# Hybrid decoder layer on one core: head 2's queries and scores placed between V rows 4 to 9, unit 2's routing two groups later, head 0's score copies ahead of two exponentials

## The chip, the cores and the metric

The kernel runs on one core of one Trainium2 chip. The metric is the device time of one execution in microseconds (us), as the median of several runs. TensorE multiplies, ScalarE applies functions and copies, VectorE does element-wise work and reductions, GpSimd here builds tables and issues the gathers, SyncE issues the plain loads. 16 DMA engines carry out the transfers of all of them.

## What is computed

One decoder layer on 256 tokens of width 1024, in float32. First a norm, a combined projection, and two kinds of attention side by side (8 heads of block attention, 4 of differential attention), an output projection and the residual. Then a second norm and the part that takes most of the time, a feed-forward layer of 16384 single-neuron experts:

```python
q = (xc @ w_query).reshape(PEER_CHUNK, PEER_HEADS, 2, PEER_D_HALF)
sc = jnp.einsum('chpd,hpnd->chpn', q, sub_keys)
s1, i1 = lax.top_k(sc[:, :, 0], PEER_TOPK)
s2, i2 = lax.top_k(sc[:, :, 1], PEER_TOPK)
cand = s1[..., :, None] + s2[..., None, :]
...
best, pos = lax.top_k(cand, PEER_TOPK)
g = jax.nn.softmax(best, axis=-1)
h = jax.nn.gelu(jnp.einsum('cd,chkd->chk', xc, u[experts]), approximate=False)
return jnp.einsum('chk,chkd->cd', h * g, v[experts])
```

Each token has 8 heads, and each head picks 16 experts: from two score vectors of 128 keys the best 16 each, from their sums the best 16 pairs. For each expert a row of `u` (1024 numbers) is multiplied with the token's vector, and a row of `v` is added to the result with the weight `gelu(...) * g`.

## The kernel before

The 256 tokens are two halves of 128, which lie on the 128 partitions. The work of the expert layer is cut into 16 **units** (half times head), each of 16 **rows**: row n of the 256 is one gathered tile of U (128 partitions x 1024, each partition its own expert's row, 512 KB) and one of V. Four rows are a **group**, so there are 64 groups, four to a unit. U tiles lie in a ring of 10 buffers, V tiles in a ring of 9.

Every engine has a program of its own, written out by hand in order, and each runs strictly in that order; semaphores join them. For the expert layer these are the steps:

- TensorE, `query(e)` (L1279): 8 matmuls (16 in the trace, which counts two passes for each) make half of a head's query, from the weights `wq[e // 2]`; `key_scores(e)` (L1274) multiplies it with the 128 keys. Event e is head e // 2 of the first half of the tokens for e under 16. `head_queries(i)` (L1294) does both events of head i in one piece: it is called for heads 0, 1 and 2 before the loop over V rows (L1363); later heads stand between V rows.
- ScalarE copies the query out of PSUM (`query_evac`, L656) for `key_scores`, and the scores for VectorE (`scores_evac`, L647). It also does the exponentials of the attention (`exponentials(b)`, L543; batches 4 to 11 belong to the second half of the tokens), the gelu of a group (`gelu(g)`, L696, on four dot products), and for each row the diagonal matrix of its weights (`diagonal(n)`, L702; a ring of 8).
- VectorE turns scores into expert numbers, in three parts (`route(u, part)`, L1004): the top keys, the top candidates, the expert numbers (`expert_ready`) and softmax inputs. It makes the dot products of a group (`dots(g)`, L1016), which wait for their U rows and free their buffers (`u_used`), and the group's weights from gelu and softmax (`weights(g)`, L1027), one group later. x is read from SBUF in groups 0 to 2 and from PSUM afterwards.
- GpSimd issues the gathers (L463): in turn g the four U rows of group g (at the start of a unit it waits for that unit's experts; each row waits for its buffer), and then the four V rows of group g - 2, which wait for V buffers freed by TensorE (`v_used`).
- TensorE multiplies each V row with its diagonal (L1372), adding into the output banks.
- SyncE loads the query weights in four portions (L396 to L404). `wq[2]` and `wq[3]` overwrite `v_sb` and `soft`, which the attention of the second half still reads, so their loads wait for its last values product (`values_done`). `wq[4]` to `wq[7]` wait for the last output projection of the second half, whose steps stand between V rows 11 to 22.

Around the change ScalarE's program for the start of the loop is: exponentials 10 and 11, two copies of probabilities, x into PSUM, squares and square root for the second half's attention output (`d_squares`, `d_deviation`), the copies of head 2's queries and scores (L721 to L724), and then `gelu(0)`. VectorE's is: routing of unit 0, attention work, `dots(0)`, first part of routing unit 1, `dots(1)`, `weights(0)`, the other two parts of unit 1, `dots(2)`, `weights(1)`, first part of unit 2. The whole loop waits for nothing else on GpSimd's side than expert numbers and free buffers.

## Time and profile before

| | us |
|---|---|
| median of 3 runs | 840.93 (838.71 to 841.11) |
| the profiled execution, as timed | 836.34 |
| its span from the first to the last instruction | 834.5 |
| TensorE busy | 679.0 (81%) |
| VectorE busy | 525.5 (63%) |
| ScalarE busy | 236.6 (28%) |
| GpSimd busy | 502.4 (60%) |
| gathers of U and V (268.47 MB), share of 16 DMA engines | 81.5% of the span |
| mean TensorE clock granted | 0.943 |

The page cuts the span into 40 equal slices of 20.9 us and gives for each the busy share of every engine, the granted clock, and the bytes that the DMA engines moved. Busy shares are averages over stages that have different limits, so a change is read from the stage in which it stands: which engine waits there, for whom, and what that engine waits for itself. In a timeline row the number in brackets is the idle time of the engine before the instruction, with the one that released it. POOL is GpSimd, DVE is VectorE, ACT is ScalarE, PE is TensorE.

### The profile page before, as it was taken

How to read it: one execution, taken by the hardware profiler on the slowest of the kernel's cores; microseconds unless marked ns; L12 is line 12 of the kernel's file. 1: busy time of each engine (PE TensorE's matmuls, PEld its weight loads, DVE VectorE, ACT ScalarE, POOL GpSimd, SP SyncE). 2: the span in 40 equal slices, each digit the busy share in tenths (PEclk: the TensorE clock that was granted, in tenths of full speed). 3: DMA queues.
4: the chain of work that ended last, by engine and by line, in shares of the span. 5: the costliest groups of instructions: out<-in, count | busy, mean ns of one | idle time of the engine just before them, and what ended most of it. 6: DMA issues, size and time to landing. Idle time of an engine off the chain costs nothing.

```text
span 834.5 us, 7478 instructions
## 1 busy us (share of the span) xinstructions
PE 679.0 (81%) x2205; PEld 369.6 (44%) x2205; DVE 525.5 (63%) x1389; ACT 236.6 (28%) x606; POOL 502.4 (60%) x533
## 2 busy tenths in 40 slices
PE   5999997469978988878888989887776667777776
PEld 4877575435435444335444445443332223333332
DVE  5565169279652867576667676657666757665454
ACT  7567244232311432311212222331212121212110
POOL 5000007447773777777777767777777776777751
PEclk9999998599997999999999999999999999999999
DMA  8955108949999999999999999999999999999994
GB/s 326 310 166 185 53 1 305 376 143 404 409 403 390 400 409 409 407 409 410 408 409 409 409 409 409 411 409 409 409 410 408 410 409 409 409 409 409 409 409 180
DMA packets 92121, 297.91 MB, mean 357 GB/s; under 512 B 8737, under 2 KB 17074, under 8 KB 92082
## 3 DMA queue, kind: packets, MB, share of 16 engines
q0 software_dynamic: 73728, 268.47, 81.5%
q1 hardware_dynamic: 18354, 28.98, 10.1%
q8 instruction: 18, 0.29, 0.1%
q14 instruction: 21, 0.17, 0.1%
HBM read 296.36 MB, written 1.05 MB: 356 GB/s over the span
## 4 chain that ended last, share of the span: by engine, by line
DMA 34%; PE 34%; POOL 15%; issue 7%; DVE 6%; ACT 4%; DVEq 0%; SPq 0%; POOLq 0%; ACTq 0%
DMA v_row<-in_peer_v_dram,expert 23%; PE bank L1372 16%; POOL u_row L446 9%; DMA u_row<-in_peer_u_dram,expert 7%; POOL v_row L457 6%; PE xg L1119 5%; PE bank L1290 4%; DMA wq<-in_peer_w_query_dram 3%; PE bank L1244 3%; DVE u_row L1023 2%; PE bank L1185 1%; PE bank L1168 1%; ACT soft L549 1%; DMA x_sb<-in_x_dram 1%; ACT L700 0%
## 5 line engine op out<-in xcount | busy, mean ns | idle before, releaser
L1372 PE MATMUL bank<-v_row,diag 128*128 128x512 f32 x1000 | 475.7, 622 | 110.8 <-DMA v_row<-in_peer_v_dram,expert 94.7
L1023 DVE CUSTOM_DVE_ANT_0 u_row<-u_row,xg 128x1024 f32<-128x1024 f32 x244 | 296.4, 1220 | 186.2 <-DMA u_row<-in_peer_u_dram,expert 178.5
L1372 PEld LDWEIGHTS bank<-v_row,diag 128*128 128x128 f32 x1000 | 189.3, 198 | 353.9 <-issue 320.1
L446 POOL DMA_INDIRECT u_row<-in_peer_u_dram,expert x256 | 246.4, 962 | 148.0 <-DVE expert L999 70.5
L457 POOL DMA_INDIRECT v_row<-in_peer_v_dram,expert x256 | 241.2, 942 | 113.3 <-issue 56.6
L1290 PE MATMUL bank<-featT,wq 128*128 128x128 f32 x512 | 68.8, 294 | 23.1 <-DMA wq<-in_peer_w_query_dram 22.2
L1290 PEld LDWEIGHTS bank<-featT,wq 128*128 128x128 f32 x512 | 68.3, 210 | 38.0 <-DMA wq<-in_peer_w_query_dram 23.2
L700 ACT ACTIVATE h_gelu<-h_dot 128x4 f32<-128x4 f32 x64 | 12.8, 202 | 251.8 <-DVE h_dot L1023 251.7
L707 ACT ACTIVATE diag<-ident,act_w 128x128 f32<-128x128 f32 x250 | 82.5, 389 | 3.6 <-DVE act_w L1036 3.6
L660 ACT ACTIVATE qT<-bank 128x128 f32<-128x128 f32 x32 | 8.9, 277 | 176.7 <-PE bank L1290 176.7
L356 POOL TENSOR_TENSOR normed<-qk_raw,t_qk_rs 128x512 f32<-128x512 f32 x4 | 4.1, 1047 | 56.6 <-DVE t_qk_rs L896 56.6
L795 DVE TENSOR_TENSOR w_lo<-w_raw,w_hi 128x2048 fp32r<-128x2048 f32 x12 | 27.8, 2327 | 7.5 <-ACT w_hi L493 7.5
L1036 DVE TENSOR_TENSOR act_w<-h_gelu,gate 128x4 f32<-128x4 f32 x64 | 10.3, 161 | 35.0 <-ACT h_gelu L700 34.4
L1119 PE MATMUL xg<-w_hi,xn_hi 128*128 128x512 f32 x72 | 29.5, 410 | 2.0 <-ACT qk_raw L529 2.0
L1244 PE MATMUL bank<-w_raw,mixT 128*128 128x512 f32 x64 | 29.6, 593 | 0.0
L1119 PE MATMUL xg<-w_hi,xn_lo 128*128 128x512 f32 x72 | 28.9, 401 | 0.0
L1119 PE MATMUL xg<-w_lo,xn_hi 128*128 128x512 f32 x72 | 28.6, 398 | 0.0
L654 ACT ACTIVATE scores<-bank 128x128 f32<-128x128 f32 x32 | 8.7, 276 | 67.4 <-PE bank L1277 67.4
L493 ACT ACTIVATE w_hi<-w_raw 128x2048 fp32r<-128x2048 f32 x12 | 22.9, 1922 | 4.9 <-DMA w_raw<-in_w_in_dram 2.3
L957 DVE MAX8 key_val<-scores 128x8 f32<-128x128 f32 x64 | 15.4, 282 | 11.0 <-ACT scores L654 11.0
L700 ACT ACT_TABLE_LOAD x17 | 21.8, 1283 | 0.3
L1023 DVE DVE_READ_ACCUMULATOR2_ANT h_dot<- 128x1 f32 x256 | 21.1, 82 | 0.0
(160 smaller groups left out, 518.0 us busy)
## 6 DMA issues: line engine op xcount, KB each, us to landing
w_raw<-in_w_in_dram SPq DMA_DIRECT2D x12, 1024.0 KB, 7.9
wq<-in_peer_w_query_dram SPq DMA_DIRECT2D x8, 1024.0 KB, 18.1
w_raw<-in_w_out_dram SPq DMA_DIRECT2D x4, 1024.0 KB, 5.1
u_row<-in_peer_u_dram,expert POOLq DMA_INDIRECT x256, 16.5
v_row<-in_peer_v_dram,expert POOLq DMA_INDIRECT x256, 16.6
x_sb<-in_x_dram SPq DMA_DIRECT2D x2, 512.0 KB, 3.8
g_row<-in_norm_g_dram SPq DMA_DIRECT2D x1, 512.0 KB, 12.9
out_dram<-y_rows SPq DMA_DIRECT2D x1, 512.0 KB, 6.7
```

The source lines that it names most:

```text
L446: pool.indirect_dma_start(u_rows[n % U_RING][:, :], None, peer_u[0], bass.IndirectOffsetOnAxis(ap=expert[:, u, s:s + 1], axis=0))\
L457: pool.indirect_dma_start(v_rows[n % V_RING][:, :], None, peer_v[0], bass.IndirectOffsetOnAxis(ap=expert[:, u, s:s + 1], axis=0))\
L493: act.activation(w_hi[:, j % W_PARTS, :, :].rearrange("p k n -> p (k n)"), w_raw[:, j % W_LOADS, :], ACT.Copy)\
L700: act.activation(h_gelu[:, u % 4, s:s + GROUP], h_dot[:, u % 4, s:s + GROUP], ACT.Gelu).then_inc(gelu_done, 1)
L707: act.activation(diag[:, m % DIAG_RING, :], ident[:, :], ACT.Copy, scale=act_w[:, u % 4, s:s + 1])\
L795: dve.tensor_tensor(w_lo[:, j % W_PARTS, :, :].rearrange("p k n -> p (k n)"), w_raw[:, j % W_LOADS, :], w_hi[:, j % W_PARTS, :, :].rearran ...
L957: at[a] = mark(dve.max(key_val[:, r2, a, top], score[a]))
L1023: dve.tensor_tensor_reduce(out=row[:, :], in0=row[:, :], in1=x_of, scale=1.0, scalar=0.0, op0=ALU.mult, op1=ALU.add, accum_out=h_dot[:, u ...
L1119: ins = mm(ps[bank][:, :], a[:, 4 * kh + k, h * P:(h + 1) * P], b[:, j % W_PARTS, k, :], start=kh == 0 and k == 0 and n == 0, stop=kh == 1 ...
L1244: ins = mm(ps[y_bank(h, c)][:, :], mixT[h][:, 4 * kh + k, :], w_raw[:, j % W_LOADS, k * COLS:(k + 1) * COLS], start=False, stop=last)
L1290: ins = mm(ps[2 + e % 2][:, 0:P], wq[i][:, k, c * P:(c + 1) * P], featT[h][:, k, :], start=k == 0, stop=k == KD - 1)
L1372: ins = mm(ps[y_bank(h, c)][:, :], diag[:, m % DIAG_RING, :], v_rows[n % V_RING][:, c * COLS:(c + 1) * COLS], start=False, stop=True, skip ...
```

## The change

Three things move; nothing is added or left out.

1. `head_queries(2)` goes away before the loop over V rows. TensorE now does `query(4)` behind V row 4, `query(5)` behind row 6, `key_scores(4)` behind row 7 and `key_scores(5)` behind row 9. ScalarE's four copies go behind the diagonals of rows 6, 8, 9 and 11, two rows later than on TensorE, as it is done for later heads.
2. The routing of unit 2, one part in each of the turns 2, 3 and 4 of VectorE's loop, now has its first part in turn 4 and the other two in turn 5.
3. `exponentials(4)` stands behind the copies of head 0's scores instead of ahead of them.

```diff
--- before.py
+++ after.py
@@ -667,9 +667,9 @@
             skT_evac(1)
             query_evac(0)
             query_evac(1)
-            exponentials(4)
             scores_evac(0)
             scores_evac(1)
+            exponentials(4)
             exponentials(5)
             act.wait_ge(late_v_done, 1)
             act.activation(v_sb[:, 0, 1, :], ps[5][:, :], ACT.Copy).then_inc(copied, 1)
@@ -718,10 +718,6 @@
                 act.activation(xg[:, c, :], scaled[:, 0, c * COLS:(c + 1) * COLS], ACT.Copy).then_inc(xg_in_psum, 1)
             d_squares(1)
             d_deviation(1)
-            query_evac(4)
-            query_evac(5)
-            scores_evac(4)
-            scores_evac(5)
             for g in range(GROUPS + 1):
                 if g < GROUPS:
                     gelu(g)
@@ -743,6 +739,15 @@
                             feat_evac(1, 0)
                             feat_evac(1, 1)
                         u, at = divmod(n - 2, TOPK)
+                        if u == 0:
+                            if at == 4:
+                                query_evac(4)
+                            if at == 6:
+                                query_evac(5)
+                            if at == 7:
+                                scores_evac(4)
+                            if at == 9:
+                                scores_evac(5)
                         if 0 <= u <= 4:
                             e = 2 * (u + 3)
                             if at == 10:
@@ -1074,8 +1079,13 @@
                 if g == 12:
                     x2_rstd(1)
                 u, at = divmod(g - 2, UNIT_GROUPS)
-                if 0 <= u and at < 3 and u + 2 < UNITS:
+                if 0 < u and at < 3 and u + 2 < UNITS:
                     route(u + 2, at)
+                if g == 4:
+                    route(2, 0)
+                if g == 5:
+                    route(2, 1)
+                    route(2, 2)
             weights(GROUPS - 1)
 
             for k, n in enumerate(ADDED_ROWS):
@@ -1344,7 +1354,6 @@
             soft_transposes(8, 11)
             values(7, 10)
             values(8, 11)
-            head_queries(2)
 
             def out_step(step):
 
@@ -1389,6 +1398,14 @@
                     x2_transposes(1)
                 if n == 57:
                     pe.wait_ge(featT_ready[0], 3)
+                if n == 4:
+                    query(4)
+                if n == 6:
+                    query(5)
+                if n == 7:
+                    key_scores(4)
+                if n == 9:
+                    key_scores(5)
                 if u <= 4:
                     e = 2 * (u + 3)
                     if at == 10:
```

The line numbers behind the change are higher by 5 to 10 than before.

On TensorE, at the end of the attention and the start of the V rows, before (the L1290 row is head 2's query, L1372 a V row):

```order
L1168 MATMUL bank<-v_sb,probsT 128x64 x8
L1155 MATMUL xg<-ident,soft 128x128 x8
L1168 MATMUL bank<-v_sb,probsT 128x64 x8
L1290 MATMUL bank<-featT_121,wq_128 128x128 x16
L1277 MATMUL bank<-skT,qT 128x128 x2
L1372 MATMUL bank<-v_row_144,diag 128x512 x2
L1372 MATMUL bank<-v_row_145,diag 128x512 x2
```

and now, from V row 3 on (L1300 is `query`, L1287 a score product, L1243 transposes, L1381 a V row; rows 0 to 2 stand right behind the values product):

```order
L1381 MATMUL bank<-v_row_147,diag 128x512 x2
L1381 MATMUL bank<-v_row_148,diag 128x512 x2
L1300 MATMUL bank<-featT_121,wq_128 128x128 x8
L1381 MATMUL bank<-v_row_149,diag 128x512 x2
L1381 MATMUL bank<-v_row_150,diag 128x512 x2
L1300 MATMUL bank<-featT_121,wq_128 128x128 x8
L1381 MATMUL bank<-v_row_151,diag 128x512 x2
L1287 MATMUL bank<-skT,qT 128x128
L1381 MATMUL bank<-v_row_152,diag 128x512 x2
L1243 MATMUL bank<-ident,scaled 128x128 x8
L1381 MATMUL bank<-v_row_144,diag 128x512 x2
L1287 MATMUL bank<-skT,qT 128x128
```

Head 2's block ahead of the V rows is gone, and its query stands in two halves behind V rows 4 and 6, its scores behind rows 7 and 9.

On ScalarE, at the end of the attention's work and the start of the groups, before (L566 is the square root, L660 and L654 the copies of queries and scores, L700 gelu, L707 diagonals):

```order
L561 ACTIVATE scaled<-bank 128x512
L566 ACT_TABLE_LOAD
L566 ACTIVATE t_d_sd<-t_d_ms 128x4
L660 ACTIVATE qT<-bank 128x128 x2
L654 ACTIVATE scores_123<-bank 128x128 x2
L700 ACT_TABLE_LOAD
L700 ACTIVATE h_gelu<-h_dot 128x4 x2
L707 ACTIVATE diag<-ident,act_w 128x128 x4
L700 ACTIVATE h_gelu<-h_dot 128x4
L707 ACTIVATE diag<-ident,act_w 128x128 x4
```

and now:

```order
L561 ACTIVATE scaled<-bank 128x512
L566 ACT_TABLE_LOAD
L566 ACTIVATE t_d_sd<-t_d_ms 128x4
L700 ACT_TABLE_LOAD
L700 ACTIVATE h_gelu<-h_dot 128x4 x2
L707 ACTIVATE diag<-ident,act_w 128x128 x4
L700 ACTIVATE h_gelu<-h_dot 128x4
L707 ACTIVATE diag<-ident,act_w 128x128 x3
L660 ACTIVATE qT<-bank 128x128
L707 ACTIVATE diag<-ident,act_w 128x128
L694 ACT_TABLE_LOAD
```

The gelu of group 0 and the diagonals of rows 0 to 3 come directly behind the square root, and the first copy for head 2 behind the diagonal of row 6.

On ScalarE, at head 0's queries and scores, before (L549 are exponentials):

```order
L660 ACTIVATE qT<-bank 128x128 x2
L549 ACT_TABLE_LOAD
L549 ACTIVATE soft,t_sums<-soft,t_nmax 128x256 x2
L654 ACTIVATE scores_123<-bank 128x128 x2
L549 ACTIVATE soft,t_sums<-soft,t_nmax 128x256 x2
```

and now:

```order
L660 ACTIVATE qT<-bank 128x128 x2
L654 ACTIVATE scores_123<-bank 128x128 x2
L549 ACT_TABLE_LOAD
L549 ACTIVATE soft,t_sums<-soft,t_nmax 128x256 x4
```

The two score copies have moved ahead of the table load and all four exponentials.

## Rows read from the trace of the kernel before

**Rows 1.** The page: GB/s in its slices, and one group of instructions on VectorE
```profile
GB/s 326 310 166 185 53 1 305 376 143 404 409 403 390 400 409 409 407 409 410 408 409 409 409 409 409 411 409 409 409 410 408 410 409 409 409 409 409 409 409 180
...
L1023 DVE CUSTOM_DVE_ANT_0 u_row<-u_row,xg 128x1024 f32<-128x1024 f32 x244 | 296.4, 1220 | 186.2 <-DMA u_row<-in_peer_u_dram,expert 178.5
```

**Rows 2.** Windows of three stretches: busy by engine, clock, DMA share, GB/s
```profile
core 0: us, PE busy (x) PEld busy (x) DVE busy (x) ACT busy (x) POOL busy (x), PEclk, DMA share, GB/s
160.00:165.00 5.00, 2.37 (x11) 2.37 (x12) 0.00 (x0) 0.00 (x0) 0.00 (x0) 0.50 1.03 394
165.00:190.00 25.00, 18.52 (x56) 9.83 (x56) 18.29 (x64) 8.11 (x20) 10.34 (x10) 0.90 0.56 182
190.00:230.00 40.00, 40.00 (x127) 20.43 (x126) 32.36 (x96) 11.05 (x32) 30.24 (x33) 1.00 1.03 409
```

**Rows 3.** Timeline of GpSimd: start, us, instruction, idle time before it
```profile
125.32 1.19 POOL L446 DMA_INDIRECT u_row<-in_peer_u_dram,expert  x1 [52.48 <-DVE expert L999]
...
157.91 0.94 POOL L457 DMA_INDIRECT v_row<-in_peer_v_dram,expert  x1 [0.30 <-issue]
...
176.91 0.93 POOL L446 DMA_INDIRECT u_row<-in_peer_u_dram,expert  x1 [18.07 <-DVE expert L999]
...
179.79 1.99 POOL L446 DMA_INDIRECT u_row<-in_peer_u_dram,expert  x1 [0.30 <-issue]
...
218.35 0.94 POOL L446 DMA_INDIRECT u_row<-in_peer_u_dram,expert  x1 [0.30 <-issue]
...
237.04 0.93 POOL L457 DMA_INDIRECT v_row<-in_peer_v_dram,expert  x1 [0.34 <-PE bank L1372]
```

**Rows 4.** Timelines of ScalarE and VectorE, 150 to 177 us
```profile
150.68 0.20 ACT L566 ACTIVATE t_d_sd<-t_d_ms 128x4 f32<-128x4 f32 x1
...
169.56 1.28 ACT L700 ACT_TABLE_LOAD   x1
...
171.16 0.16 DVE L1036 TENSOR_TENSOR act_w<-h_gelu,gate 128x4 f32<-128x4 f32 x1 [20.33 <-ACT h_gelu L700]
...
176.47 0.18 DVE L999 SCALAR_TENSOR_TENSOR expert<-pair_idx 128x16 uint32<-128x16 f32 x1
```

**Rows 5.** Timeline of TensorE: head 2's queries, V rows 4 on, half queries
```profile
162.63 5.74 PE L1290 MATMUL bank<-featT,wq 128*128 128x128 f32 x32 [12.19 <-DMA wq<-in_peer_w_query_dram]
...
182.70 10.55 PE L1372 MATMUL bank<-v_row,diag 128*128 128x512 f32 x20 [3.76 <-ACT diag L707]
...
197.40 1.95 PE L1290 MATMUL bank<-featT,wq 128*128 128x128 f32 x16
...
199.18 1.88 PE L1372 MATMUL bank<-v_row,diag 128*128 128x512 f32 x4
...
254.50 3.78 PE L1290 MATMUL bank<-featT,wq 128*128 128x128 f32 x16 [10.01 <-DMA wq<-in_peer_w_query_dram]
```

**Rows 6.** Landing: query weights 2; the last two; V 155-160 us; U 125-131 us
```profile
DMA to landing us min/median/max: 12.1/12.1/12.1
...
DMA to landing us min/median/max: 39.5/39.7/39.8
...
DMA to landing us min/median/max: 9.6/10.3/11.0
...
DMA to landing us min/median/max: 4.6/5.2/6.1
```

**Rows 7.** Timelines of ScalarE and VectorE around head 0's scores, and head 2's second
```profile
113.40 0.28 ACT L660 ACTIVATE qT<-bank 128x128 f32<-128x128 f32 x1 [1.51 <-PE bank L1290]
...
119.72 0.60 ACT L675 ACTIVATE v_sb<-bank 128x512 f32<-128x512 f32 x1 [2.33 <-PE bank L1119]
...
169.26 0.28 ACT L654 ACTIVATE scores<-bank 128x128 f32<-128x128 f32 x1 [0.35 <-PE bank L1277]
...
116.50 0.49 DVE L957 MAX8 key_val<-scores 128x8 f32<-128x128 f32 x2 [2.90 <-ACT scores L654]
...
124.22 0.18 DVE L999 SCALAR_TENSOR_TENSOR expert<-pair_idx 128x16 uint32<-128x16 f32 x1
```

## The prediction

> **What bounds the kernel now.** I read the slices of the page first, to see when which resource is full. From about 190 us to 815 us the transfers move 390 to 411 GB/s, mostly 409, in every slice [rows 1]: that stretch is bound by the DMA engines, at 0.5243 MB (128 x 1024 x 4 bytes) / 409 GB/s = 1.28 us for a gathered row of U or V. Such a stretch gets shorter only by starting earlier or by losing a gap. There is one gap: the slice at 167 to 188 us stands at 143 GB/s [rows 1]. Cut out by windows, 165 to 190 us moved 182 GB/s instead of 409, so 25 x (1 - 182/409) = **13.9 us of transfer time are missing** [rows 2].
>
> Next I asked who starved the queue. GpSimd issues all gathers, in program order. After v7 at 157.91 us it idles 18.07 us until u16, released by expert numbers from VectorE [rows 3]. VectorE itself sat 20.33 us at its first activation weights, for the gelu of group 0 on ScalarE [rows 4]. ScalarE had its last square root done at 150.88 us; next in its program stand the copies of head 2's queries and scores, and only behind them the gelu, whose table load began at 169.56 us [rows 4]. TensorE's query(4) waited for query weights 2: 12.19 us, to 162.63 us [rows 5]. These weights overwrite values still read by the last values product, so their load can only be issued at 150.5 us, and it took 12.1 us beside the gathers [rows 6]. So one late load holds ScalarE, through it VectorE, through it GpSimd, and in the end all transfers, although no U row of unit 1 needs head 2's query.
>
> **Part 1: head 2's queries move behind V rows 4 to 9.** Nothing is removed: 32 query matmuls, 4 score matmuls and 4 copies are still there. Now after the square root ScalarE loads the gelu table and runs gelu. Before, table load to activation weights was 169.56 to 171.16 = 1.60 us [rows 4], so the weights come at 150.88 + 1.60 = 152.5 us, 18.7 us earlier. Candidates and experts of unit 1 follow in 176.65 - 171.16 = 5.5 us [rows 4], to 158.0 us. GpSimd is done with v7 at 158.85 us. The wait of 18.07 us vanishes, down to the 0.3 us between gathers.
>
> What is late next? The transfers issued by then still need time: a gather issued at 155 to 160 us landed after 10.3 us against 5.2 us in the stream's first 6 us [rows 6]. I take the smallest landing there, 4.6, as unloaded and the largest, 11.0, as loaded: **6.4 us of queued work** cover small delays of GpSimd. The next 32 gathers took from 176.91 to 218.35 us, 41.4 us [rows 3], for 32 x 1.28 = 41.0 us of transfer, so the cover stays about constant. u16 to u19 need dot products 6 to 9: the first eight are done when VectorE's wait begins, at 150.8 us [rows 4], the next two come 18.7 us earlier, like the weights. I take the whole gap as gained: **-13.9 us**. Its ends: no gain at all if the wait merely finds a new place (a rival below), and 17.8 us (the whole wait of GpSimd less 0.3) if transfers followed the issues one for one. The value stays at the missing bytes, since the transfers, not the issues, set the end.
>
> **The dot products beside the gathers.** The dot products of group 2 still read x from SBUF and run while u16 to u19 are issued; beside them one gather took 1.99 us instead of 0.93 [rows 3], 1.1 us more, which the 41.4 us contain. The Trainium skill (GPSIMD Engine Reference, Specifications) says that GpSimd's SBUF interfaces are shared with VectorE and that VectorE instructions with two SBUF inputs contend. Taken strictly, all four gathers would pay the 1.1 us, 3.2 us more than here, and unhidden the sum would be 12.6 us instead of 15.8; by the rows the cost is the 1.1 us, and hidden. The trace agrees with the rule in kind, not for all four.
>
> **Part 2: unit 2's routing two groups later.** It needs head 2's scores, which now hang behind V row 9. V row 4 began at 182.70 us once its diagonal was there [rows 5]; 18.7 us earlier is 164.0. From there to the second score product TensorE has 6 V rows, two queries, eight transposes and two small products. A V row is 1.7 us (x4 row, 1.88 with its drain), a query half of 16 matmuls 1.8 [rows 5]: 10.3 + 3.6 + 1.3 (12 small matmuls at a sixteenth of a half query) = 15.2 us, and 2 us more because the five rows of before took 10.55 instead of 8.6 us as the clock rose [rows 5]. Scores at 181.2, copied 181.8. V rows 8 and 9 land before that, since their gathers follow u16's, which comes at 158.3 us (158.0 and the issue) instead of 176.91, 18.6 us earlier. VectorE then needs the key tops (three parts took 116.50 to 124.40 = 7.9 us [rows 7], less 5.5 = 2.4), four dot products of 1.22 us [rows 1] and 5.5 us for the other two parts: experts of unit 2 at 181.8 + 12.8 = 194.6 us. GpSimd wants them for u32 at 158.3 + 41.4 = 199.7 us, and with the cover 206.1 would do. VectorE may wait some 6 us for the scores; cost 0, hidden by 5 us in GpSimd's order and 6.4 us of queued transfers. If that cover were gone, each us late would cost one.
>
> **Part 3: TensorE and the V ring.** From V row 4 at 182.70 us TensorE works nearly without a gap [rows 2, 5], and at 237.04 us v31 takes the slot of V row 22, for which GpSimd had waited 0.34 us [rows 3]. That is 54.3 us; the change puts 4.0 us into it (two queries, two scores). Row 22: 164.0 + 54.3 + 4.0 = 222.3 us; GpSimd wants it at 237.04 - 18.6 = 218.4. It waits 3.9 us, under the cover of 6.4: cost 0, but this is the thinnest cover of all. Load waits at the later query weights go with it: the four loads are issued behind V row 22's neighbours, as before.
>
> **Part 4: head 0's scores ahead of the exponentials.** Before, ScalarE copied the two scores after a table load and two exponentials, and VectorE idled 2.90 us until 116.50 [rows 7]. Now the first copy follows the query copy of 113.40 + 0.28, ends near 113.9, and the second starts 0.35 us later for the score product (the gap at 169.26 us is that product) [rows 7]: 114.25 to 114.5, and VectorE starts near 114.6, 1.9 us earlier, and so do the experts of unit 0 and the first gather, at 125.32 us before [rows 3]. GpSimd's other gate there, the late value product, ends at 119.7 us, before the experts of 122.5, and stays hidden. The exponentials come about 0.8 us later, hidden by ScalarE's idle time of 2.33 us before 119.72 [rows 7]. The stream starts 1.9 us earlier and is full: **-1.9 us**, between 0 (if it only lengthens a queue) and 2.9 (the whole idle time). I gave part 1 none of this head start.
>
> **Sum.** 13.9 + 1.9 = 15.8 us. The profiled execution took 836.34 us (span 834.5), so 820.5 for it; the median of the three runs, 840.93, lies 4.6 us above it, and with that gap kept: **825.1 us**.
>
> **Rivals.**
> (a) *The clock takes it back.* At 160 to 165 us the granted clock was 0.50, the 1.2 GHz level, after 12 us without matmuls [rows 2]; before, the query block ran there and the V rows after it at 2.4 GHz. Now V rows 0 to 3 come first, then a wait for the next diagonal. A half query took 3.78 us at the low level against 1.95 [rows 5]. If all work from row 4 to 9 runs low, it costs 15.2 us more: row 22 at 237.5 against 218.4 + 6.4 = 224.8, a loss of 12.7 us, so 837.8 us. Against it: before, the clock was back within 5.7 us of query matmuls. The Trainium skill (TensorE: Matmul & The Clock Gate, Part 1) says that the throttled clock is the default and activity lifts it; by that rule the thin V rows 0 to 3 would leave TensorE low, which is this rival. Chance 0.06; half its price lies inside my range.
> (b) *Head 0 brings nothing*, because something else holds GpSimd's first gather or the head start is lost before 160 us: 827.0. Chance 0.10.
> (c) *The wait only changes its name.* ScalarE or VectorE meets another wait before unit 1's experts, and GpSimd stays at u16 until about 177 us: 840.9. Every operand on that path is done by 150.9 us in the trace, so 0.04.
> (d) *Slower: head 2's weights land late.* Place: query(4) behind V row 4, now with an uninterrupted gather stream beside the load. From landing to unit 2's experts I count 27 us: 13.5 on TensorE (15.2 less V row 4), then 0.6 and 12.8. Landing by 179 us is harmless (206.1 - 27); from 195 us on the idle time eats all 15.8 us. The load took 12.1 us beside the same gathers, but the last of four took 39.8 us [rows 6], which from 150.5 gives 190.3 and still a gain of 4.6. Beyond that it turns over: at 50 us, 200.5, it is 21.4 - 15.8 = +5.6, 846.5 us. For speaks the fuller queue, against that the first of its group took 12.1 us, and that V rows would stop being issued and give way. Chance 0.03.
>
> **Numbers.** Forecast 0.77, (a) 0.06, (b) 0.10, (c) 0.04, (d) 0.03. The range begins at 821.0, where GpSimd's whole 17.8 us and 1.9 would count (821.2), and ends at 832.0, which takes in (b), half of (a) and what is lost if the thin cover of part 3 is gone (3.9 us) together with the 2 us of clock. A measurement of this kernel can tell about 0.3%, 2.5 us, from no change: faster 0.93 (forecast, (a), (b)), same 0.04, slower 0.03.
>
> **What would show it.** The slices hold 400 GB/s and more from 155 us on, with no hole. GpSimd has no wait over 4 us before u32, the first gather is issued near 123.4 us, the weights of group 0 come near 152 us, ScalarE's wait for the first query of head 2 remains but releases nobody. VectorE waits some 6 us for head 2's scores near 180 us. The forecast is wrong if GpSimd shows a new wait of over 6.4 us for expert numbers or for V slots, or if the last gather's landing does not move by some 16 us.

## The result, and the profile after

| | before | the change |
|---|---|---|
| median, us | 840.33 (838.71 to 841.11, 4 runs) | 820.44 (820.02 to 821.02, 4 runs) |
| ratio of the times | | 0.9766 [0.9749, 0.9783] |
| profiled execution, us | 836.34 | 820.27 |
| its span, us | 834.5 | 818.5 |
| mean TensorE clock granted | 0.943 | 0.943 |

The change makes the kernel 2.3% faster, 19.9 us between the medians. Forecast were 825.1 us and a range of 821.0 to 832.0, so the direction is right, and the time lies 0.6 us below the range. Against the one profiled execution of before the gain is 16.0 us of span; the sum of the prediction was 15.8. The two statements differ by what separates that execution from the median, and that is where the forecast went wrong.

The page of the change: GB/s in its 40 slices (20.5 us each), and the queue of the gathers:

```profile
GB/s 326 322 155 174 83 1 298 391 402 409 408 395 392 406 409 409 409 409 409 409 409 409 409 409 409 411 409 409 410 409 409 410 409 410 409 409 409 409 408 166
...
q0 software_dynamic: 73728, 268.47, 82.8%
```

From the ninth slice, at 164 us, on every one but the last is at 392 GB/s or more, mostly 409, and the sixth to ninth slices read 1, 298, 391, 402 where [rows 1] had 1, 305, 376, 143: the hole is gone. (The prediction asked for 400 and more from 155 us on; three slices, the eighth, twelfth and thirteenth, stand at 391 to 395.) The packets of the gathers now take 82.8% of the 16 DMA engines' span, 81.5% before. The windows, with the columns of [rows 2]:

```profile
core 0: us, PE busy (x) PEld busy (x) DVE busy (x) ACT busy (x) POOL busy (x), PEclk, DMA share, GB/s
120.00:165.00 45.00, 35.52 (x156) 25.84 (x153) 39.16 (x110) 18.87 (x53) 31.92 (x29) 0.77 0.89 325
165.00:190.00 25.00, 25.00 (x116) 15.75 (x115) 18.42 (x61) 8.42 (x22) 18.78 (x20) 1.00 1.03 404
190.00:230.00 40.00, 37.41 (x91) 16.49 (x89) 29.36 (x87) 8.98 (x26) 28.76 (x31) 1.00 1.03 407
230.00:270.00 40.00, 31.18 (x95) 16.71 (x96) 22.28 (x70) 11.92 (x30) 22.66 (x24) 0.87 1.04 394
```

165 to 190 us now moves 404 GB/s instead of 182, and TensorE is busy through it. GpSimd's timeline, as [rows 3]:

```profile
122.94 1.19 POOL L446 DMA_INDIRECT u_row<-in_peer_u_dram,expert  x1 [49.02 <-DVE expert L1004]
...
154.81 0.94 POOL L457 DMA_INDIRECT v_row<-in_peer_v_dram,expert  x1 [0.30 <-issue]
...
157.50 0.94 POOL L446 DMA_INDIRECT u_row<-in_peer_u_dram,expert  x1 [1.75 <-DVE expert L1004]
...
160.38 1.99 POOL L446 DMA_INDIRECT u_row<-in_peer_u_dram,expert  x1 [0.31 <-issue]
...
198.97 0.94 POOL L446 DMA_INDIRECT u_row<-in_peer_u_dram,expert  x1 [0.30 <-issue]
...
219.96 0.94 POOL L457 DMA_INDIRECT v_row<-in_peer_v_dram,expert  x1 [2.24 <-PE bank L1381]
```

u16, at 157.50 us, waited 1.75 us for its expert numbers instead of 18.07; u32 came at 198.97 us without a wait for its experts; v31, at 219.96 us, waited 2.24 us for V row 22's slot. Behind u32 there is one longer wait, for a V slot as well, here and then in before:

```profile
242.94 0.94 POOL L457 DMA_INDIRECT v_row<-in_peer_v_dram,expert  x1 [7.13 <-PE bank L1381]
...
260.60 0.94 POOL L457 DMA_INDIRECT v_row<-in_peer_v_dram,expert  x1 [7.73 <-PE bank L1372]
```

It is over the 6.4 us that the prediction named as a sign of being wrong, but it is not new: it only comes 17.7 us sooner, as part 3 had it for the waits behind the later query weights. ScalarE and then VectorE, as [rows 4, 7]:

```profile
113.76 0.28 ACT L654 ACTIVATE scores<-bank 128x128 f32<-128x128 f32 x1 [0.35 <-PE bank L1287]
...
150.02 1.28 ACT L700 ACT_TABLE_LOAD   x1
```

```profile
114.14 0.49 DVE L962 MAX8 key_val<-scores 128x8 f32<-128x128 f32 x2 [1.04 <-ACT scores L654]
...
151.62 0.16 DVE L1041 TENSOR_TENSOR act_w<-h_gelu,gate 128x4 f32<-128x4 f32 x1 [1.58 <-ACT h_gelu L700]
...
179.10 0.49 DVE L962 MAX8 key_val<-scores 128x8 f32<-128x128 f32 x2 [6.20 <-ACT scores L654]
```

Head 0's second score copy now ends at 114.04 us, ahead of any exponential, and VectorE waits 1.04 us for it instead of 2.90. The gelu's table load begins at 150.02 us, straight behind the square root, instead of 169.56, and the first activation weights follow at 151.62. TensorE, as [rows 5], and then the landing of query weights 2, as the first of [rows 6]:

```profile
152.27 8.60 PE L1381 MATMUL bank<-v_row,diag 128*128 128x512 f32 x16 [2.58 <-ACT diag L707]
...
163.29 1.98 PE L1381 MATMUL bank<-v_row,diag 128*128 128x512 f32 x4 [2.42 <-ACT diag L707]
...
165.11 1.95 PE L1300 MATMUL bank<-featT,wq 128*128 128x128 f32 x16
...
178.37 0.38 PE L1287 MATMUL bank<-skT,qT 128*128 128x128 f32 x2
...
217.81 1.88 PE L1381 MATMUL bank<-v_row,diag 128*128 128x512 f32 x4
```

```profile
DMA to landing us min/median/max: 14.2/14.2/14.2
```

The load was issued at 149.7 us and landed 14.2 us later, at 163.9, before TensorE came to the query at 165.11: the load that had held everything holds nobody.

### The profile page after: what moved, and what is told of

Its sections match the earlier page's. It is cut to its first block, busy times and chain, and to the rows that moved or that the text cites. A ratio compares the mean times of both kernels' runs of the same rounds, so it can differ in the third digit from the quotient of the medians.

```text
span 818.5 us, 7478 instructions
## 1 busy us (share of the span) xinstructions
PE 679.8 (83%) x2205; PEld 367.6 (45%) x2205; DVE 527.3 (64%) x1389; ACT 236.7 (29%) x606; POOL 503.2 (61%) x533
## 3 DMA queue, kind: packets, MB, share of 16 engines
q0 software_dynamic: 73728, 268.47, 82.8%
## 4 chain that ended last, share of the span: by engine, by line
DMA 42%; PE 31%; POOL 12%; issue 6%; DVE 5%; ACT 4%; DVEq 0%; SPq 0%; POOLq 0%; ACTq 0%
DMA v_row<-in_peer_v_dram,expert 23%; DMA u_row<-in_peer_u_dram,expert 16%; PE bank L1381 13%; POOL u_row L446 8%; PE xg L1129 4%; POOL v_row L457 4%; PE bank L1300 4%; PE bank L1254 3%; DVE u_row L1028 3%; DMA wq<-in_peer_w_query_dram 2%; PE bank L1195 1%; PE bank L1178 1%; ACT soft L549 1%; PE bank L1129 1%; DMA x_sb<-in_x_dram 0%
## 5 line engine op out<-in xcount | busy, mean ns | idle before, releaser
L1381 PE MATMUL bank<-v_row,diag 128*128 128x512 f32 x1000 | 481.3, 627 | 107.5 <-DMA v_row<-in_peer_v_dram,expert 93.1
L1381 PEld LDWEIGHTS bank<-v_row,diag 128*128 128x128 f32 x1000 | 190.5, 200 | 353.0 <-issue 319.0
L700 ACT ACTIVATE h_gelu<-h_dot 128x4 f32<-128x4 f32 x64 | 12.8, 202 | 246.8 <-DVE h_dot L1028 246.7
L707 ACT ACTIVATE diag<-ident,act_w 128x128 f32<-128x128 f32 x250 | 82.7, 389 | 4.1 <-DVE act_w L1041 4.1
L1300 PEld LDWEIGHTS bank<-featT,wq 128*128 128x128 f32 x512 | 65.1, 201 | 26.2 <-issue 15.4
L1300 PE MATMUL bank<-featT,wq 128*128 128x128 f32 x512 | 65.4, 284 | 10.9 <-DMA wq<-in_peer_w_query_dram 10.0
L660 ACT ACTIVATE qT<-bank 128x128 f32<-128x128 f32 x32 | 8.9, 278 | 166.4 <-PE bank L1300 166.4
L654 ACT ACTIVATE scores<-bank 128x128 f32<-128x128 f32 x32 | 8.9, 278 | 67.8 <-PE bank L1287 67.8
L962 DVE MAX8 key_val<-scores 128x8 f32<-128x128 f32 x64 | 15.3, 281 | 13.3 <-ACT scores L654 13.3
## 6 DMA issues: line engine op xcount, KB each, us to landing
v_row<-in_peer_v_dram,expert POOLq DMA_INDIRECT x256, 16.3
g_row<-in_norm_g_dram SPq DMA_DIRECT2D x1, 512.0 KB, 13.3
```

Source lines behind the costliest of these rows:

```text
L700: act.activation(h_gelu[:, u % 4, s:s + GROUP], h_dot[:, u % 4, s:s + GROUP], ACT.Gelu).then_inc(gelu_done, 1)
L707: act.activation(diag[:, m % DIAG_RING, :], ident[:, :], ACT.Copy, scale=act_w[:, u % 4, s:s + 1])\
L962: at[a] = mark(dve.max(key_val[:, r2, a, top], score[a]))
L1300: ins = mm(ps[2 + e % 2][:, 0:P], wq[i][:, k, c * P:(c + 1) * P], featT[h][:, k, :], start=k == 0, stop=k == KD - 1)
L1381: ins = mm(ps[y_bank(h, c)][:, :], diag[:, m % DIAG_RING, :], v_rows[n % V_RING][:, c * COLS:(c + 1) * COLS], start=False, stop=True, skip ...
```

## The experiments

Three sets, each on another chip, and each with before run beside it on the same one: before's median was 839.7 us (23 runs, 836.4 to 841.6) in the first, 913.6 (29 runs, 905.1 to 922.3) in the second, 840.4 (13 runs, 837.3 to 841.8) in the third. Ratios are to before of the same set. The GB/s of five windows are used more than once; all are from the window view, which the rows shown here are samples of:

| GB/s at us | 120-165 | 165-190 | 190-230 | 230-270 | 270-300 |
|---|---|---|---|---|---|
| before, first trace | 299 | 182 | 409 | 396 | 402 |
| e1, before again | 290 | 157 | 398 | 400 | 397 |
| the change | 325 | 404 | 407 | 394 | 408 |
| e2, queries only | 292 | 403 | 408 | 393 | 408 |
| f2, load later | 305 | 334 | 310 | 356 | 400 |

**Before once more (e1).** No edit. The change had gained more than the profiled execution of before could lose; the question is whether the stall itself is longer in a usual execution.

> The kernel before, unchanged, for more executions and a second trace. Its traced execution took 836.3 us while its timed ones took 838.7 to 841.1; the change's five-odd executions all took 820.0 to 821.0. Theory T1: the landing of query weights 2, which holds everything up in the kernel before, varies from execution to execution and was early in the first trace (12.1 us). Then a trace of about 840 us shows it landing after about 16 us, GpSimd's wait before the 17th U row near 22 us instead of 18.07, and the rest as before. Rival T2: the whole stretch of transfers varies; then the load lands after 12 to 13 us and the difference of some 4 us is spread over the slices after 190 us or stands in the time before the first gather.

Measured: 839.92 us (838.91 to 842.81, 12 runs), ratio 1.0004 [0.9992, 1.0016]; this profiled execution took 839.96 us, span 838.1. The landing of query weights 2, then VectorE and GpSimd in the timeline:

```profile
DMA to landing us min/median/max: 15.9/15.9/15.9
```

```profile
174.96 0.16 DVE L1036 TENSOR_TENSOR act_w<-h_gelu,gate 128x4 f32<-128x4 f32 x1 [24.00 <-ACT h_gelu L700]
...
125.45 1.19 POOL L446 DMA_INDIRECT u_row<-in_peer_u_dram,expert  x1 [52.50 <-DVE expert L999]
...
180.72 0.94 POOL L446 DMA_INDIRECT u_row<-in_peer_u_dram,expert  x1 [21.70 <-DVE expert L999]
```

And three windows of it:

```profile
120.00:165.00 45.00, 24.84 (x140) 20.57 (x138) 28.67 (x81) 15.37 (x43) 26.56 (x24) 0.72 0.81 290
165.00:190.00 25.00, 16.84 (x57) 10.36 (x58) 14.49 (x55) 7.84 (x19) 7.46 (x7) 0.84 0.47 157
190.00:230.00 40.00, 40.00 (x126) 20.38 (x125) 32.59 (x99) 11.33 (x33) 30.25 (x33) 0.99 1.01 398
```

The first gather stands where it stood (125.45 us against 125.32), so the start of the kernel is not the difference. The load took 15.9 us instead of 12.1 for the same megabyte issued at the same point: 3.8 more. VectorE's wait is 24.00 instead of 20.33, GpSimd's 21.70 instead of 18.07: 3.6 more. The span is 3.6 us longer. So of the 4.6 us between the first trace and the median 3.6 were a longer stall at the very place that the change removes. The last 1.0 us is within what so few runs scatter: 840.93 was the median of three runs, and that of the 23 runs of this set is 839.7.

**Without the head 0 part (e2).** The change with its third part undone:

```diff
             query_evac(1)
+            exponentials(4)
             scores_evac(0)
             scores_evac(1)
-            exponentials(4)
             exponentials(5)
```

> The change without its head 0 part (exponentials 4 stand ahead of head 0's score copies again). T1: the late load is off the path, so the scatter is small (under 1.5 us) and the time is that of the change plus 1.9: 822.3 us, 18 us under the kernel before as timed, though only 13.9 of transfer time were missing in its trace. T2: 840.3 - 13.9 = 826.4 us with the scatter of before. Rival for head 0 (it brings nothing): 820.4 us.

Measured: 823.39 us (822.73 to 824.93, 5 runs), ratio 0.9809 [0.9790, 0.9829]. GpSimd's first gather and VectorE's first wait for scores:

```profile
125.27 1.19 POOL L446 DMA_INDIRECT u_row<-in_peer_u_dram,expert  x1 [52.52 <-DVE expert L1004]
...
116.46 0.49 DVE L962 MAX8 key_val<-scores 128x8 f32<-128x128 f32 x2 [2.91 <-ACT scores L654]
```

VectorE's wait is back at 2.91 us. The move of head 2's queries brings most of the gain alone, 16.3 us; the head 0 part adds 3.0 us by the medians (forecast 1.9). By the traces the two are 12.9 and 3.1 us: e2's span is 821.6. Expected were 822.3 us with less than 1.5 us between the runs if the load's scatter goes with the wait, 826.4 if it stays. The median is 1.1 us over the first and 3.0 under the second, and the five runs lie within 2.2 us, so the scatter is smaller than before's but not as small as expected.

**Only the head 0 part (e3).** Before, with only the score copies put ahead:

```diff
             query_evac(1)
-            exponentials(4)
             scores_evac(0)
             scores_evac(1)
+            exponentials(4)
             exponentials(5)
```

> The kernel before with head 0's score copies ahead of exponentials 4, nothing else. The late load stays on the path. The first gather comes 1.9 us earlier, but the stream then stops for the late load as before, so what counts is how much earlier the last values product lets that load be issued: T1 says between 0 and 1.9 us of gain, about 1.2 (TensorE idled 1.17 us for the mixing of VectorE there), so near 839 us, with a scatter of over 1.5 us. T2 says that the scatter and the 4 us belong to this part: about 835 us and a small scatter.

Measured: 838.42 us (834.47 to 840.46, 12 runs), ratio 0.9987 [0.9972, 1.0001]. VectorE and GpSimd:

```profile
115.36 0.49 DVE L957 MAX8 key_val<-scores 128x8 f32<-128x128 f32 x2 [1.04 <-ACT scores L654]
...
124.17 1.19 POOL L446 DMA_INDIRECT u_row<-in_peer_u_dram,expert  x1 [50.60 <-DVE expert L999]
...
181.04 0.94 POOL L446 DMA_INDIRECT u_row<-in_peer_u_dram,expert  x1 [23.01 <-DVE expert L999]
```

VectorE's wait is 1.04 us as in the change and the first gather is 1.3 us earlier than in e1, but this execution's span, 838.7 us, is no shorter: query weights 2 took 16.0 us, and GpSimd's wait for unit 1's experts took back what the earlier start had given, 23.01 us. As long as the late load ends the stall, an earlier stream mostly makes the wait longer; the 1.3 us between the medians can't be told from nothing. The scatter stays too: 12 runs lie within 6.0 us.

**The load later in the change (e4, e5, f2).** These take away the margin of the load to learn from where it costs. In e4 SyncE waits for four V rows, in e5 and f2 for twenty U rows, before it issues query weights 2:

```diff
+            sp.wait_ge(v_used, 4)
             query_weights(2)
```

```diff
+            sp.wait_ge(u_used, 20)
             query_weights(2)
```

> The change, but query weights 2 and 3 are issued only when V row 3 has been multiplied (near 161 us instead of 149.5), so they land 12 to 17 us later than in the change, near 173 to 178 us. Theory of the cover: landing by 179 us costs nothing, so 820.4 to 821.5 us; TensorE waits for the load behind V row 4 by some 8 to 13 us and VectorE waits as much longer for the scores. Rival (the load is still on the path): each us late costs one, about 830 us or more.

Measured for e4: 827.43 us (823.83 to 829.28, 4 runs), ratio 0.9863 [0.9840, 0.9887]; the profiled execution was the shortest, 823.83 us, span 822.0. In it the load was issued at 161.1 us and landed 10.3 us later. TensorE, GpSimd and VectorE:

```profile
171.50 3.78 PE L1301 MATMUL bank<-featT,wq 128*128 128x128 f32 x16 [5.95 <-DMA wq<-in_peer_w_query_dram]
...
214.78 0.94 POOL L458 DMA_INDIRECT v_row<-in_peer_v_dram,expert  x1 [2.50 <-PE bank L1382]
...
187.66 0.49 DVE L963 MAX8 key_val<-scores 128x8 f32<-128x128 f32 x2 [8.54 <-ACT scores L655]
```

Landing at 171.4 us, well before the 179 us that the prediction called harmless, cost 3.5 us in this trace and 7 us by the medians; the three longer runs have no trace. The four runs lie 5.5 us apart, where those of the change lie 1.0 us apart: once the load costs, the scatter is back. The row shows how: GpSimd waits for V slots, here 2.50 us for one of them, and not for experts.

> The change, but query weights 2 and 3 are issued only when the dot products of U rows 0 to 19 are done (near 173 us), so they land near 185 to 189 us. In the run with the load at 161 us the load landed 22 us after the change's issue time and the time rose by 7 us as timed and 3.5 as traced, with GpSimd waiting for V slots and not for expert numbers. So the first cover to go is the V ring (part 3 of the prediction), not the experts. Theory V: TensorE behind V row 4 stands still until about 187 us instead of 165, some 22 us, of which the cover takes about 6 to 8: 834 to 837 us, with GpSimd's longest waits at V rows 14 and 15. Theory X (expert numbers of unit 2 bind, my rival d): idle time 187 + 27 - 206 = 8 us, 828 us, and the longest wait is at U row 32.

e5 ran in the second set: 908.88 us (10 runs), ratio 0.9953 [0.9912, 0.9993]. Everything there was slower, before too. One window shows it:

```profile
300.00:780.00 480.00, 372.70 (x1041) 179.73 (x1042) 274.95 (x802) 99.93 (x291) 306.60 (x324) 0.90 0.95 358
```

The main stretch moved 358 GB/s instead of 409, and VectorE had idle times from about 140 us on for which the trace names no other work. A verdict of a few us can't be taken from it, so the same kernel ran again in the third set as f2:

> The same kernel as the one with the load issued after the dot products of U rows 0 to 19, once more, for a chip at 409 GB/s. In the disturbed set the longest wait of GpSimd (14.68 us) was for a V slot, as theory V says. Theory V: 834 to 837 us, GpSimd's longest wait at V rows 14 or 15. Theory X (expert numbers of unit 2 bind): 828 us, longest wait at U row 32.

Measured for f2: 838.06 us (834.43 to 840.18, 10 runs), ratio 0.9973 [0.9957, 0.9989]; profiled execution 839.43, span 837.6. The load was issued at 174.2 us and landed at 186.1. TensorE and GpSimd, then two windows:

```profile
186.11 3.78 PE L1301 MATMUL bank<-featT,wq 128*128 128x128 f32 x16 [19.52 <-DMA wq<-in_peer_w_query_dram]
...
192.76 0.94 POOL L458 DMA_INDIRECT v_row<-in_peer_v_dram,expert  x1 [15.42 <-PE bank L1382]
```

```profile
165.00:190.00 25.00, 5.47 (x21) 4.27 (x20) 9.13 (x17) 0.20 (x2) 9.37 (x10) 0.62 0.91 334
190.00:230.00 40.00, 40.00 (x140) 21.46 (x140) 25.85 (x95) 14.98 (x40) 23.53 (x26) 0.98 0.85 310
```

Nearly the whole gain is gone with a landing at 186.1 us, and again the wait stands at a V slot: 15.42 us. With the table, the transfers that are missing against the change are (45 x 20 + 25 x 70 + 40 x 97 + 40 x 38 + 30 x 8) / 409 = 20.3 us; the span is 19.1 us longer. That unit 2's experts would decide (820.5 + 186.1 - 179 = 827.6 us by the prediction's threshold) is refuted; that the V ring decides holds in kind, 1 us over its upper end. The scatter is back here too, 5.8 us over 10 runs.

**Before with its load later (e6).** The opposite test: if before's time follows the landing, a load held back there must cost as much as it is late.

```diff
+            sp.wait_ge(u_landed[5], 32)
             query_weights(2)
```

> The kernel before, but query weights 2 and 3 are issued only when U row 15 has landed (near 160 to 162 us instead of 150.5). With less queued they need less time to land (7.7 us unloaded, some 9 to 11 here): 170 to 172 us, against 162.6 in the first trace and 166.5 in the second. T1 (the load's landing holds everything, each us one us): 840 + 171 - 166 = 843 to 847 us. Rival (something else ends the wait): 840 us.

Measured, in the second set: 917.22 us (911.48 to 920.39, 10 runs), ratio 1.0047 [1.0004, 1.0091], so 3.6 us longer by the medians. It points the expected way, but it is no test of the question, though. TensorE's last values product, for which the load waits in every version, ended only at 158.07 us in this trace (150.44 in before's first), and the load was issued at 158.10 and landed after 5.4 us, at 163.5, no later than in the two traces of before (162.6 and 166.5). So in this trace the added wait held nothing back, and what the 3.6 us are stays open. GpSimd stood 5.84 us for the same product before V row 4, a wait that the description of its loop leaves out. That the time follows the landing rests on the two traces of before and that of e3, and for the change on e4 and f2.

**Unit 2's routing one group later instead of two (e7, f3).** The change with `route(2, 0)` at group 3 and the other parts at group 4. VectorE then meets the wait for head 2's scores one group earlier.

```diff
-                if g == 4:
+                if g == 3:
                     route(2, 0)
-                if g == 5:
+                if g == 4:
                     route(2, 1)
                     route(2, 2)
```

> The change with unit 2's routing one group later than before instead of two: first part in turn 3, the others in turn 4. VectorE then waits for head 2's scores from about 168 us to 179, 11 us instead of 6, and the dot products of U rows 16 to 19 and the weights of V rows 12 to 15 are held back by it: dot products until about 186 us where GpSimd wants the slots of rows 16 to 19 at 181 to 186 us, weights of V row 12 until about 186.5 where TensorE comes to it at 184.7. Theory (both are under the cover of queued transfers): 820.4 to 822 us. Rival (no cover left): 3 us or more over the change, 823.5 us and up.

e7, in the second set: 903.78 us (899.32 to 911.39, 12 runs), ratio 0.9890 [0.9854, 0.9926]. Again in the third set:

> The same kernel as the one with unit 2's routing one group later instead of two, once more. In the disturbed set VectorE waited 20.89 us for the scores, and GpSimd 11.93 us at a U row for a slot that dot products free. Theory (under the cover): 820.4 to 822 us. Rival (no cover left for dot products held back by VectorE's wait): 823.5 us and up, with a wait of GpSimd at a U row.

Measured for f3: 819.77 us (818.10 to 820.50, 4 runs), ratio 0.9760 [0.9730, 0.9789], against 0.9769 for the change beside it. VectorE and GpSimd:

```profile
180.81 0.49 DVE L962 MAX8 key_val<-scores 128x8 f32<-128x128 f32 x2 [11.91 <-ACT scores L654]
...
184.65 0.94 POOL L446 DMA_INDIRECT u_row<-in_peer_u_dram,expert  x1 [3.02 <-DVE h_dot L1028]
...
223.78 0.94 POOL L457 DMA_INDIRECT v_row<-in_peer_v_dram,expert  x1 [2.50 <-PE bank L1381]
```

VectorE stands 11.91 us and GpSimd is held 3.02 us, and the time does not change: the queued transfers cover it, as they cover 2.50 us at v31. So one group later would have done as well. Turn 2, where before has it, was not open: the routing there would wait for scores whose copies stand behind the diagonals of rows 9 and 11, these need `weights(2)`, and VectorE makes that only in turn 3, behind the routing. This is read from the program; no run has it.

**The change once more (f1).** No edit, in the third set.

> The change, unchanged, beside the three below. On a chip whose transfers run at 409 GB/s: 820 to 821 us. In the set of runs before this one the kernel before took 913.6 us and its transfers moved 358 GB/s between 300 and 780 us instead of 409; if that comes again, this run says what the change is worth there: the bytes cost more time, the removed gap does not, so the gain should stay between 14 and 20 us.

Measured: 820.46 us (819.98 to 820.97, 4 runs), ratio 0.9769 [0.9743, 0.9795]. Its first gather came at 124.21 us, 1.3 us later than in the first trace of the change, and the span was 818.8: the end did not follow. Most of the head start was gone by u16, which came at 157.62 us here and at 157.50 there: in the change it had to wait 1.75 us for unit 1's experts, in f1 it came after the usual 0.30 us.

**The tail (e8, f4).** At the end of the change GpSimd waits for V buffers though the U buffers are empty:

```profile
800.96 0.94 POOL L457 DMA_INDIRECT v_row<-in_peer_v_dram,expert  x1 [4.14 <-PE bank L1381]
...
803.45 1.08 POOL L457 DMA_INDIRECT v_row<-in_peer_v_dram,expert  x1 [0.31 <-PE bank L1381]
...
812.53 1.96 PE L1381 MATMUL bank<-v_row,diag 128*128 128x512 f32 x4 [1.80 <-DMA v_row<-in_peer_v_dram,expert]
```

The edit puts V rows 252 to 255 into U buffers 6 to 9; nothing else differs.

```diff
+        def v_place(n):
+            if n >= GATHERS - 4:
+                k = n - GATHERS + U_RING
+                return u_rows[k], u_landed[k], 16 * (GATHERS // U_RING + 1)
+            return v_rows[n % V_RING], v_landed[n % V_RING], 16 * (n // V_RING + 1)
...
+                if n >= GATHERS - 4:
+                    pool.wait_ge(u_used, GATHERS - 6)
```

> The change, and the last four V rows (252 to 255) are gathered into the U buffers of U rows 246 to 249, which are free by 787 us, instead of V buffers that TensorE and VectorE free only at 796 to 803 us. With the stream now without a hole, its end is what is left: the last three gathers are issued at 800.96 to 803.45 us after a wait of 4.14 us, and the last lands 8.9 us later. Theory: the last one can be issued near 799.2 us, so the end comes up to 4.3 us earlier: 816 to 818 us. Rival (the queue of transfers is full anyway and the landing does not move): 820.4 us.

e8, in the second set: 900.46 us (896.11 to 903.56, 6 runs), ratio 0.9849 [0.9795, 0.9904]. In the third set:

> The same kernel as the one whose last four V rows go into U buffers, once more. Theory: the last gather can be issued near 799 us instead of 803.45, so 816 to 818 us. Rival (the queue is full anyway): 820.4 us.

Measured for f4: 820.04 us (819.07 to 820.45, 4 runs), ratio 0.9761 [0.9734, 0.9788]. Its last gather and TensorE's last V row:

```profile
799.06 0.94 POOL L468 DMA_INDIRECT u_row<-in_peer_v_dram,expert  x1 [0.30 <-issue]
...
812.54 1.96 PE L1394 MATMUL bank<-u_row,diag 128*128 128x512 f32 x4 [1.80 <-DMA u_row<-in_peer_v_dram,expert]
```

The last gather is issued 4.4 us earlier and TensorE's last row starts at the same 812.5 us as in the change. GpSimd's wait at the end costs nothing; what delays the last landing stays open. No kernel that ran is clearly faster than the change.

## Why the prediction was right, and where it was not

**Part 1 (13.9 us): right.** The weights of group 0 came at 151.62 us (forecast 152.5), u16 at 157.50 (158.3), and the 32 gathers from u16 to u32 took 41.47 us (41.4). The account closes for both traces of before when all five windows are counted. Against the first: (45 x 26 + 25 x 222 - 40 x 2 - 40 x 2 + 30 x 6) / 409 = 16.5 us, span 16.0. Against e1: (45 x 35 + 25 x 247 + 40 x 9 - 40 x 6 + 30 x 11) / 409 = 20.1 us, span 19.6. The first window holds the earlier stream of part 4, the second the hole. This account is good to 1 or 2 us, not better: for f1 against the change it gives 1.2 us and the span 0.3, for e4 5.1 and 3.5.

**That the sum of 15.8 us met 16.0 is in part luck.** By e2's trace part 1 was worth 12.9 us, 1.0 less than forecast, and part 4 3.1 us, 1.2 more, and the two errors cancel. With one trace of each they are smaller than what separates two traces of before (3.6 us), so neither is known to 1 us.

**The dot products beside the gathers: price as forecast and hidden, the reading of the four gathers not.** The gather at 160.38 us took 1.99 us, as the one at 179.79 of [rows 3], the one before it 1.33, the others 0.94. But the dot products ran from 158.05 to 162.71 us: u16 was issued at 157.50, mostly ahead of them, and u19 at 162.68, behind them, so the two gathers that ran wholly beside them were both slower, and so it was in before (1.33 us at 178.15). The stricter reading of the Trainium skill's sentence (GPSIMD Engine Reference, Specifications), every gather beside such an instruction, fits these four; it fails for the dot products of group 1, 142.69 to 147.38 us, where the V gather at 143.82 took 0.94 us and the next, at 145.06, 1.97.

**Part 2 (0 us): right, with more room than I gave it.** V row 4 began at 163.29 us (164.0) and the second score product at 178.37 (181.2): the 2 us for the clock were not needed. VectorE waited 6.20 us near 180 us, as forecast (some 6). f3 shows that even 11.91 us there cost nothing.

**Part 3 (0 us): right for this landing.** Row 22 was done at 219.7 us (222.3), and v31 waited 2.24 us (3.9) under the cover. That this was the thinnest cover of all is what e4 and f2 confirm.

**Part 4 (1.9 us): its wait right, its worth a little low.** VectorE's wait fell from 2.90 to 1.04 us, 1.86. In the company of part 1 it is worth 3.0 us by the medians of e2 and the change; alone, 1.3 us by the medians of e3 and before, which can't be told from nothing. The 1.1 us beyond the wait are not explained: e2 and f1 differ by 1.1 us at the first gather, by 1.5 at u16 (159.13 and 157.62 us) and by 2.8 in the span, while f1 and the first trace of the change differ by 1.3 at the first gather and by 0.3 in the span. So that a head start passes to the end one for one is not what these traces show.

**The last line of the sum failed.** "With that gap kept" carried over the 4.6 us between the profiled execution and the median, as if they belonged to the whole program. Most of them belonged to the stall: e1 has them in the landing of query weights 2 (12.1 us in the first trace, 15.9 and 16.0 in e1 and e3), and everything behind passed the 3.8 us on, as 3.6 us of span. Hardly anything is left once nobody waits for the load: the eight runs of the change (f1 among them) lie within 1.0 us, 23 of before, in the first set, within 5.2, and the scatter returns in e4 (5.5 us) and f2 (5.8 us), where the load is made to cost. Without the 4.6 us the sum is 820.5, and 820.44 is the median. The low end of the range, 821.0, rested on the same step. Had I asked where the 4.6 us could come from, one term of the path was a single transfer beside a full queue, and the rows already showed how unlike such transfers are ([rows 6]: 12.1 us for this one, 39.8 for the last of four); what it varies by goes when the wait goes.

**Rival (a), the clock: not seen.** V rows 0 to 3 took 8.60 us for 16 matmuls, and from 140 to 155 us the granted clock was 0.50, the 1.2 GHz level; but from 155 to 160 us it was 0.97, from 160 to 190 us 1.00, the 2.4 GHz level, and the half query at 165.11 took 1.95 us. The Trainium skill's rule (TensorE: Matmul & The Clock Gate, Part 1), that activity lifts the clock, agrees with this; that four V rows are not activity enough was my reading, and the trace has it otherwise. Nor did the low level in before begin with the 12 us without matmuls: the clock stood at 0.50 from 140 us on, while TensorE was busy through to 150. Where TensorE had stood idle longer the low level came back: in e4, after 5.95 us, and in f2, after 19.52 us, the half query took 3.78 us.

**Rival (b)** is refuted by e2 for the two parts together; alone, in e3, the head 0 part brings nothing that can be measured. **(c)** is refuted by the timeline.

**Rival (d), the late weights: place right, threshold wrong, though it did not occur.** I followed the landing to unit 2's experts and called 179 us harmless. The same delay also moves every V row behind it, and that cover is thinner. From the change's trace: TensorE reached the query at 165.11 us, and of 6.4 us of queued transfers v31 had used 2.24, so a delay beyond 4.2 us costs. For e4 that gives 171.50 - 165.11 = 6.4, plus 1.8 for the half query and 0.4 for the two V rows behind it at the lower clock (3.98 us in its timeline against 3.60), less 4.2 = 4.4 us (3.5 in its trace); for f2 21.0 + 1.8 + 0.9 - 4.2 = 19.5 us (19.1). So by this estimate the landing is harmless until about 169 us, not 179. In the traces of kernels that don't hold it back it came between 159.8 us (f1) and 166.9 (f4), which leaves 2 to 9 us in hand and is thin: in f3 it landed at 166.7 us and TensorE already waited 0.80 us for it, without cost. My own figures would have shown it: part 3 left 6.4 - 3.9 = 2.5 us of cover, and rival (d) never used it.

## What to carry to other kernels

One profiled execution is one draw of everything on its path that varies. When a change takes a wait off the path, that wait's scatter goes too: don't carry the distance between trace and median over, ask first which term of the path can vary, and look whether it is the one being removed.

A delay has several consumers. Price it at each ring and queue that it reaches, and take the thinnest cover for the threshold; a slack that one term has used up is not there for the next. And an earlier start is worth little or nothing ahead of a wait that ends with something else (e3). Once that wait was gone it was worth 3.0 us by the medians, but how much reaches the end depends on the next wait (u16 in the change and in f1).

## What the runs showed beside this

- The same 1 MB load at the same point of the program, beside the same gathers, landed after 12.1 us in before's first trace, 15.9 in e1, 16.0 in e3, 15.3 in e2, 14.2 in the change, 11.9 in f1 and 16.4 in f3. What sets it within that range was not found.
- In the second set the gathers moved 358 GB/s from 300 to 780 us where all other traces have 409, and before took 913.6 us. No run shows why. The Trainium skill (DMA: Bandwidth & Descriptors, Bandwidth) says that a core gets about 358 GB/s when the other core of its memory domain streams as well; the figure agrees with the window, but whether another core was at work can't be seen.
- An early stop of GpSimd's issuing does not bring the end nearer: in f4 the last gather, issued 4.4 us sooner, landed 13.3 us later instead of 8.9, at the same 812.4 us. From 804 to 808 us the change moved 312 GB/s and f4 only 129, from 808 to 812 us 35 and 26. So both end in a trickle, and its last four us hold 0.14 and 0.10 MB, about a quarter and a fifth of one gathered row. 26 GB/s is about a sixteenth of 409 (25.6), so one DMA engine of the 16 may still have had work when the others were done; that is an estimate, no view shows the engines singly, and it was not tested.
